# Five seven-product units in seven of ten gate and up half-pairs, their loop written out, and first loads in another order

## The chip, the cores and the metric

The kernel runs on one core of one Trainium2 chip. The metric is the device time of one launch in microseconds (us). The engines are named as in the profile: PE is TensorE, DVE is VectorE, ACT is ScalarE, POOL is GpSimd, and SP is SyncE, which here only issues DMAs.

## What is computed

One residual block on x of 256 tokens by 2048 features, all in float32:

```python
f = swiglu(rmsnorm(h, ffn1_pre_g), ffn1_w_gate, ffn1_w_up, ffn1_w_down)   # 2048 -> 5632 -> 2048
h = h + 0.5 * rmsnorm(f, ffn1_post_g)
u = rmsnorm(h, mix_pre_g)
z = u @ w_in                                  # 2048 -> 5120: lru_x, lru_gate, sc_b, sc_c, sc_x
xc = causal_dwconv(lru_x, conv_w, conv_b)
y_lru = rg_lru(xc, w_r, b_r, w_i, b_i, lam) * gelu(lru_gate)   # 8 heads: w_r, w_i are 128x128 each
y_sc = sc_b * causal_dwconv(sc_c * sc_x, sc_conv_w)
h = h + rmsnorm(concat(y_lru, y_sc) @ w_out, mix_post_g)
h = h + 0.5 * rmsnorm(swiglu(rmsnorm(h, ffn2_pre_g), ...), ffn2_post_g)
```

where `swiglu(x) = (silu(x @ w_gate) * (x @ w_up)) @ w_down`. All matrices are read from the chip's memory once.

## The kernel before

**Precision.** A float32 product is made of three matmuls: each operand is split into a rounded part (hi, made by ACT as a cast) and the rest (lo, made by DVE as raw minus hi), and `three` (L1735, L1736, L1737) adds hi·hi, hi·lo and lo·hi in one bank. So each weight that reaches PE has had one ACT pass and one DVE pass.

**Gate and up.** Of the 11 column chunks of 512, chunk 0 is done plainly (`first_chunk`, `group`). The other 10 chunks are five pairs. A pair of 1024 columns is done for w_gate (a "half", c even) and then for w_up (c odd): HALVES = 10 halves, c = 0 to 9. A half has GP = 8 units, p = 0 to 7; a unit is 2 row blocks (of 128) by 2 column blocks (of 512) of weights, times 2 token blocks. This 2x2x2 block product is done either plainly, with 8 products, so 24 matmuls, or by the Winograd form of Strassen's scheme with 7 products, so 21 matmuls ("seven-product unit"). `SEVEN[c]` lists the units of half c that are done with seven.

A seven-product unit needs three more weight blocks, U2, V4 and V3, which are sums of the raw ones. They cost two DVE instructions (`half_sums`, L1220 and L1222), an ACT cast (`sums_hi`, L824) and a DVE subtraction (`sums_lo`, L1228). One of the raw blocks is a sum of two, which POOL makes by an accumulating DMA (`pair_sums`, L675).

**Order on DVE** in a half (`half_steps`): the seven bank sums that empty the last half's PSUM banks (`bank_sums`), `half_lo` of unit 1; then for each unit in turn `half_sums` if it is a seven, `half_lo` (L1207), `sums_lo` if it is a seven. In an even half (c = 2, 4, ...) `pair_hidden` of the previous pair lies between `half_sums` and `half_lo` of units 2 and 4 (L1172, two instructions). At the end it does unit 0 of the next half. Three waits tie DVE to PE: `half_sums` waits until PE is through with the seven-product unit two before it (`two_back`, since the sums have two buffers), `bank_sums` waits for the last matmuls of the half, and in even halves ACT's cast `sums_hi` of unit 6 lies behind two PSUM copies (`pair_copy`) of transposes that PE does after units 3 to 6 (`pair_transpose`, 4 transposes each).

**Buffers.** The raw, hi and lo weights have four places; unit p uses place p % 4. Places 0 and 1 (`u_raw0`) lie where the ring of the plain chunks lay, places 2 and 3 (`u_raw1`) where `resid` lay. So in half 0 the loads of units 0 and 1 wait for `lo_ready` of the plain chunk's late groups, and those of units 2 and 3 for the squares of all blocks of `resid` (`blk_sq`) and, in the second FFN, for its copy to memory (`resid_kept`).

**Loops.** Half 0 and half 9 are written out. Halves 1 to 8 are a hardware loop on each of SP, ACT, DVE and PE: `Fori` with two turns, TURN = 4 halves in each turn. Waits in it are on register values.

**Mixer.** The columns of w_in are 10 chunks of 8 groups (`load_chunk`), each group one 512 KB load in a ring of four slots. SP issues loads in the order of its program; before the second chunk (q == 1) it waits for `fg_done` (the gains of the first FFN's last bank), then loads the gain row of the mixer's norm, broadcast to 1 MB (`gpost`), and the heads w_r and w_i (512 KB each). The heads are first used on PE at chunk 3, group 6; the gain in the output projection.

Of the kernel before, what the change touches and what calls it, by code (L numbers as in the profile page):

```python
# [22 lines left out]
def hybrid_block_kernel(nc, x, f1_pre, f1_wg, f1_wu, f1_wd, f1_post, mix_pre, w_in, conv_w, conv_b,  # L23
# [67 lines left out]

# [3 lines left out]
    TURN = 4  # L95
    SEVEN = [(2, 4, 6)] + [(0, 2, 3, 4, 6) if c % 2 else (0, 2, 4, 6) for c in range(1, HALVES)]
# [3 lines left out]
    turn_sevens = first_seven[1 + TURN] - first_seven[1]  # L100
# [20 lines left out]
    assert FC == 2 * PAIRS + 1 and HALVES == 2 + 2 * TURN and NS % 2 == turn_sevens % 2 == 0  # L121
# [16 lines left out]
    def lin(q, a, b):  # L138

        it, c = q  # L140
        return a * c + b if isinstance(it, int) else it * (TURN * a) + (a * c + b)
# [10 lines left out]
    with ctx:  # L152
# [241 lines left out]
        def turns(q, a, b):  # L394

            it, c = q
            return b if isinstance(it, int) else it * a + b

# [3 lines left out]
        def seven_count(f, q, p):  # L402
            return turns(q, turn_sevens, NS * f + seven_place(q, p) + 1)

        def sums_count(f, q, p, back=0):
            return turns(q, 2 * turn_sevens, 2 * (NS * f + seven_place(q, p) + 1) - back)
# [4 lines left out]
        def pair_count(f, q, p):  # L411
            units = [p in SEVEN[c] for c in range(HALVES)]
            return turns(q, 16 * sum(units[1:1 + TURN]), 16 * (sum(units) * f + sum(units[:q[1] + 1])))
# [4 lines left out]
        def raw_count(f, q, p):  # L418
            halves = [sum(raw_loads(c, p % 4 + 4)) for c in range(HALVES)]
            return turns(q, sum(halves[1:1 + TURN]),  # L420
                         sum(halves) * f + sum(halves[:q[1]]) + sum(raw_loads(q[1], p)))
# [48 lines left out]
        def _(sync):  # L470
# [25 lines left out]
            def ffn(f):  # L496
# [15 lines left out]
                with sync.Fori(0, (HALVES - 2) // TURN) as it:  # L512
                    for c in range(1, 1 + TURN):
                        load_half(f, (w_gate, w_up)[c % 2], (it, c))
# [34 lines left out]
            def load_half(f, w, q):  # L549
                it, c = q  # L550
                for p in range(GP):
                    if q[1] == 0 and p < 4:
# [9 lines left out]
                    def cols(b, n):  # L562
                        return (slice(first + b * W, first + b * W + n * W) if isinstance(it, int)
                                else ds(it * (TURN * W) + (first + b * W), n * W))
# [18 lines left out]

            X_LOADS = ((0, 1), (2,), (3,), (4, 5, 6, 7), (), (), (), ())
            ffn(0)
            for q, (kind, jc) in enumerate(Z):
                if q == 1:
                    sync.wait_ge(fg_done, TOK * NC)
                    load_gain(mix_post)
                    sync.wait_ge(w_used, starts["in"])  # L590
# [1430 lines left out]
```

## Time and profile before

| | us |
|---|---|
| runs of the kernel | 1741.73, 1742.92, 1745.69; median 1742.92 |
| the profiled execution's own time | 1742.19 |
| its span, first to last instruction | 1740.2 |
| PE busy | 1716.8 |
| DVE busy | 1460.6 |
| ACT busy | 993.1 |
| granted PE clock | 0.999 |

Busy times are unions of the instructions' spans. A matmul's end is modelled: one of 128x512 stands as 0.39 us long, while the next one starts 0.23 us after it, so "busy" includes overlap, and the distance between starts is the time that a matmul takes of PE.

### The profile page before, as it was taken

Reading aid. Unit: us, or ns where it says so; the run is one execution under the profiler, and the core shown is the slowest. Engines: PE = TensorE matmul, PEld = TensorE weight load, DVE = VectorE, ACT = ScalarE, POOL = GpSimd, SP = SyncE. Lnnn points to the kernel's source line nnn. Section 1 sums busy time; section 2 is a strip of 40 time slices with the busy share of each in tenths; the row PEclk is TensorE's granted clock in tenths of the full one; section 3 lists DMA queues with packets and bytes.
Section 4 is the critical chain, followed back from the end, with each engine's and each line's share of the span. In section 5 each row is a group of like instructions: output and inputs, shape, how many; then the busy total and the mean of one; then the engine's idle time right before and its main releaser. Section 6 shows DMA issues by size and latency. Waiting matters only on the chain.

```text
span 1740.2 us, 21509 instructions
## 1 busy us (share of the span) xinstructions
PE 1716.8 (99%) x7712; PEld 1417.0 (81%) x7712; DVE 1460.6 (84%) x1286; ACT 993.1 (57%) x951; POOL 183.5 (11%) x175
## 2 busy tenths in 40 slices
PE   8999999999999999999999999999999999999998
PEld 6788888888888888788888878788888888888886
DVE  6899999999989877755685558999989999989787
ACT  6665656555656454656654447565656565755453
POOL 5210000000000000100000018011010111000010
PEclk9999999999999999999999999999999999999999
DMA  7788878787767688665565656887877787677775
GB/s 233 229 230 234 227 227 242 221 241 219 227 198 235 221 231 265 197 205 175 163 194 180 194 181 226 231 241 227 237 224 228 232 233 233 194 227 229 227 226 206
DMA packets 150825, 382.38 MB, mean 220 GB/s; under 512 B 12620, under 2 KB 14804, under 8 KB 149972
## 3 DMA queue, kind: packets, MB, share of 16 engines
q1 hardware_dynamic: 133716, 350.33, 61.9%
q0 software_dynamic: 16992, 30.94, 11.3%
q8 instruction: 49, 0.80, 0.2%
q14 instruction: 36, 0.29, 0.1%
q10 hardware_dynamic: 32, 0.01, 0.0%
HBM read 377.03 MB, written 4.19 MB: 219 GB/s over the span
## 4 chain that ended last, share of the span: by engine, by line
PE 90%; DVE 3%; POOL 2%; DMA 2%; issue 1%; ACT 1%; DVEq 0%; SPq 0%; ACTq 0%
PE ps L1735 22%; PE ps L1737 22%; PE ps L1736 22%; PE ps L1633 7%; PE ps L1635 7%; PE ps L1634 7%; PE ps L1730 1%; POOL x L638 1%; DVE u_lo L1207 1%; DMA u_raw<-in_ffn_w_gate 1%; DVE w_lo L1090 1%; DMA raw<-in_w_in 1%; DMA u_raw<-in_ffn_w_up 1%; PE ps L1944 1%; DVE tsum L1222 0%
## 5 line engine op out<-in xcount | busy, mean ns | idle before, releaser
L817 ACT CAST u_hi<-u_raw 128x2048 fp32r<-128x2048 f32 x160 | 305.9, 1912 | 167.2 <-DMA u_raw<-in_ffn_w_gate 87.8
L1207 DVE TENSOR_TENSOR u_lo<-u_raw,u_hi 128x2048 fp32r<-128x2048 f32 x160 | 366.4, 2290 | 9.2 <-ACT u_hi L817 5.3
L1090 DVE TENSOR_TENSOR w_lo<-raw,w_hi 128x1024 fp32r<-128x1024 f32 x156 | 199.8, 1288 | 135.1 <-ACT w_hi L718 132.9
L718 ACT CAST w_hi<-raw 128x1024 fp32r<-128x1024 f32 x160 | 166.6, 1051 | 139.5 <-PE ps L1635 112.3
L1735 PE MATMUL ps<-u_hi,xT_hi 128*128 128x512 f32 x608 | 236.8, 390 | 0.0
L1737 PE MATMUL ps<-u_hi,xT_lo 128*128 128x512 f32 x608 | 236.8, 389 | 0.0
L1736 PE MATMUL ps<-u_lo,xT_hi 128*128 128x512 f32 x608 | 236.6, 389 | 0.0
L979 ACT CAST d_hi<-d_raw 128x2048 fp32r<-128x2048 f32 x80 | 153.0, 1912 | 117.9 <-DMA d_raw<-in_ffn_w_down 117.9
L1420 DVE TENSOR_TENSOR d_lo<-d_raw,d_hi 128x2048 fp32r<-128x2048 f32 x80 | 183.0, 2289 | 18.4 <-ACT d_hi L979 15.1
L824 ACT CAST t_hi<-tsum 128x1536 fp32r<-128x1536 f32 x88 | 130.6, 1484 | 102.4 <-DVE tsum L1222 101.5
L1633 PE MATMUL ps<-w_hi,xT_hi 128*128 128x512 f32 x448 | 179.1, 400 | 4.2 <-DVE xT_lo L1128 3.2
L1735 PE MATMUL ps<-d_hi,hT_all 128*128 128x512 f32 x460 | 179.1, 389 | 0.0
L1737 PE MATMUL ps<-d_hi,hT_all 128*128 128x512 f32 x460 | 179.0, 389 | 0.0
L1736 PE MATMUL ps<-d_lo,hT_all 128*128 128x512 f32 x460 | 178.9, 389 | 0.0
L1635 PE MATMUL ps<-w_hi,xT_lo 128*128 128x512 f32 x448 | 175.3, 391 | 0.0
L1634 PE MATMUL ps<-w_lo,xT_hi 128*128 128x512 f32 x448 | 175.1, 391 | 0.0
L1228 DVE TENSOR_TENSOR t_lo<-tsum,t_hi 128x1536 fp32r<-128x1536 f32 x88 | 154.2, 1752 | 20.7 <-ACT t_hi L824 20.7
L1736 PEld LDWEIGHTS ps<-u_lo,xT_hi 128*128 128x128 f32 x608 | 114.1, 188 | 24.1
L1737 PEld LDWEIGHTS ps<-u_hi,xT_lo 128*128 128x128 f32 x608 | 114.1, 188 | 24.1
L1735 PEld LDWEIGHTS ps<-u_hi,xT_hi 128*128 128x128 f32 x608 | 114.1, 188 | 24.0
L1735 PE MATMUL ps<-u_hi,xf 128*128 128x512 f32 x320 | 128.7, 402 | 3.9 <-DVE u_lo L1207 3.6
L1737 PE MATMUL ps<-u_hi,xf 128*128 128x512 f32 x320 | 124.9, 390 | 0.0
(203 smaller groups left out, 3039.9 us busy)
## 6 DMA issues: line engine op xcount, KB each, us to landing
d_raw<-in_ffn_w_down SPq DMA_DIRECT2D x50, 1024.0 KB, 6.8
u_raw<-in_ffn_w_gate SPq DMA_DIRECT2D x42, 1024.0 KB, 5.2
raw<-in_w_in SPq DMA_DIRECT2D x80, 512.0 KB, 3.7
u_raw<-in_ffn_w_up SPq DMA_DIRECT2D x30, 1024.0 KB, 5.1
u_raw<-in_ffn_w_up SPq DMA_DIRECT2D x100, 256.0 KB, 4.1
u_raw<-in_ffn_w_up SPq DMA_DIRECT2D x50, 512.0 KB, 3.7
u_raw<-in_ffn_w_gate SPq DMA_DIRECT2D x76, 256.0 KB, 4.3
u_raw<-in_ffn_w_gate SPq DMA_DIRECT2D x38, 512.0 KB, 3.7
```

The lines of the kernel that those rows point to most:

```text
L718: sc.copy(w_hi[:, s], raw[:, s]).then_inc(hi_ready, 1)
L817: sc.copy(unit(u_hi, p), unit(u_raw, p)).then_inc(unit_hi, 1)
L1090: ve.tensor_tensor(w_lo[:, s], raw[:, s], w_hi[:, s].bitcast(f32), ALU.subtract).then_inc(lo_ready, 1)
L1207: ve.tensor_tensor(unit(u_lo, p), unit(u_raw, p), unit(u_hi, p).bitcast(f32), ALU.subtract).then_inc(unit_lo, 1)
L1228: ve.tensor_tensor(t_lo[:, u], tsum[:, u], t_hi[u][:].bitcast(f32), ALU.subtract).then_inc(t_lo_done, 1)
L1420: ve.tensor_tensor(d_lo[n][:], d_raw[n][:], d_hi[n][:].bitcast(f32), ALU.subtract).then_inc(d_lo_done, 1)
L1633: te.matmul(dst, xh, w_hi[:, s, k], start=start and k == 0, stop=False)
L1634: te.matmul(dst, xh, w_lo[:, s, k], start=False, stop=False)
L1635: last = te.matmul(dst, xl, w_hi[:, s, k], start=False, stop=stop and k == GK - 1)
L1735: te.matmul(dst, xs[0], hi, start=start, stop=False)
L1736: te.matmul(dst, xs[0], lo, start=False, stop=False)
L1737: return te.matmul(dst, xs[1], hi, start=False, stop=stop)
```

## The change

The list of seven-product units is another one: halves 2 and 6 keep four, half 0 keeps three, and the other seven have five (before, only odd halves had five). In each FFN two more units, unit 3 of halves 4 and 8, are done with seven products. With that, the four `Fori` loops over halves 1 to 8 are written out as Python loops, and the register arithmetic (`turns`, `lin`) falls away. In half 0 SP issues the loads of units 2 and 3 ahead of those of units 0 and 1. In the mixer the heads are loaded one at a time, at group 4 of chunk 1 and group 2 of chunk 2, and the gain row at the start of chunk 3.

```diff
     PAIRS = (FC - 1) // 2
     HALVES = 2 * PAIRS
     UNITS = HALVES * GP
-    TURN = 4
-    SEVEN = [(2, 4, 6)] + [(0, 2, 3, 4, 6) if c % 2 else (0, 2, 4, 6) for c in range(1, HALVES)]
+    SEVEN = [(2, 4, 6)] + [(0, 2, 4, 6) if c in (2, 6) else (0, 2, 3, 4, 6) for c in range(1, HALVES)]
...
     def lin(q, a, b):
-        it, c = q
-        return a * c + b if isinstance(it, int) else it * (TURN * a) + (a * c + b)
+        return a * q[1] + b
...
         def seven_count(f, q, p):
-            return turns(q, turn_sevens, NS * f + seven_place(q, p) + 1)
+            return NS * f + seven_place(q, p) + 1
...
                 load_half(f, w_gate, (0, 0))
-                with sync.Fori(0, (HALVES - 2) // TURN) as it:
-                    for c in range(1, 1 + TURN):
-                        load_half(f, (w_gate, w_up)[c % 2], (it, c))
+                for c in range(1, HALVES - 1):
+                    load_half(f, (w_gate, w_up)[c % 2], (0, c))
                 load_half(f, w_up, (0, HALVES - 1))
...
             def load_half(f, w, q):
                 it, c = q
-                for p in range(GP):
-                    if q[1] == 0 and p < 4:
+                for p in ((2, 3, 0, 1, 4, 5, 6, 7) if c == 0 else range(GP)):
+                    if c == 0 and p < 4:
                         old = Place(starts[f"up{f + 1}"])
                         if p < 2:
                             sync.wait_ge(lo_ready, old.count(2 * GP - 3 + 2 * p))
...
+            HEADS_LOAD = {(1, 4): (0, w_r), (2, 2): (1, w_i)}
             X_LOADS = ((0, 1), (2,), (3,), (4, 5, 6, 7), (), (), (), ())
             ffn(0)
             for q, (kind, jc) in enumerate(Z):
-                if q == 1:
-                    sync.wait_ge(fg_done, TOK * NC)
-                    load_gain(mix_post)
-                    sync.wait_ge(w_used, starts["in"])
-                    for m, w in enumerate((w_r, w_i)):
+                for j in range(GP):
+                    if (q, j) in HEADS_LOAD:
+                        m, w = HEADS_LOAD[q, j]
+                        sync.wait_ge(w_used, starts["in"])
                         sync.dma_start(w_ri[:, m], w[0].rearrange("h d e -> d h e")).then_inc(heads_in, 16)
-                load_chunk(Place(starts["in"] + GP * q), w_in_v, Z_COL[kind] // W + jc, range(GP))
+                    elif (q, j) == (3, 0):
+                        sync.wait_ge(fg_done, TOK * NC)
+                        load_gain(mix_post)
+                    load_chunk(Place(starts["in"] + GP * q), w_in_v, Z_COL[kind] // W + jc, [j])
...
-                with dve.Fori(0, (HALVES - 2) // TURN) as it:
-                    for c in range(1, 1 + TURN):
-                        half_steps(f, (it, c))
+                for c in range(1, HALVES - 1):
+                    half_steps(f, (0, c))
```

ACT's and PE's loops are written out in the same way as DVE's, and the other counters lose their `turns` as `seven_count` does.

## Rows read from the trace of the kernel before

**Rows 1.** Page, part 1: busy us (share of the span), instructions.

```profile
PE 1716.8 (99%) x7712; PEld 1417.0 (81%) x7712; DVE 1460.6 (84%) x1286; ACT 993.1 (57%) x951; POOL 183.5 (11%) x175
```

**Rows 2.** Timeline, TensorE (start us, us): first matmuls of two units, transposes between.

```profile
205.70 0.39 PE L1735 MATMUL ps<-u_hi,xf 128*128 128x512 f32 x1
...
246.50 0.60 PE L1730 MATMUL ps<-ident,hid 128*128 128x128 f32 x4
246.86 0.48 PE L1735 MATMUL ps<-u_hi,xf 128*128 128x512 f32 x1
```

**Rows 3.** Timeline, VectorE, from one even unit 4 to the next half's.

```profile
203.23 2.29 DVE L1207 TENSOR_TENSOR u_lo<-u_raw,u_hi 128x2048 fp32r<-128x2048 f32 x1
205.44 1.75 DVE L1228 TENSOR_TENSOR t_lo<-tsum,t_hi 128x1536 fp32r<-128x1536 f32 x1
207.10 2.28 DVE L1207 TENSOR_TENSOR u_lo<-u_raw,u_hi 128x2048 fp32r<-128x2048 f32 x1
209.31 0.69 DVE L1220 TENSOR_TENSOR tsum<-u_raw 128x512 f32<-128x512 f32 x1
...
211.29 2.29 DVE L1207 TENSOR_TENSOR u_lo<-u_raw,u_hi 128x2048 fp32r<-128x2048 f32 x1
...
241.93 2.29 DVE L1207 TENSOR_TENSOR u_lo<-u_raw,u_hi 128x2048 fp32r<-128x2048 f32 x1
```

**Rows 4.** Timeline, VectorE: its longest idle time; a unit behind the loop.

```profile
254.47 1.76 DVE L1228 TENSOR_TENSOR t_lo<-tsum,t_hi 128x1536 fp32r<-128x1536 f32 x1 [2.20 <-ACT t_hi L824]
...
449.82 0.69 DVE L1220 TENSOR_TENSOR tsum<-u_raw 128x512 f32<-128x512 f32 x1 [0.24 <-PE ps L1737]
...
451.88 2.29 DVE L1207 TENSOR_TENSOR u_lo<-u_raw,u_hi 128x2048 fp32r<-128x2048 f32 x1
```

**Rows 5.** Timeline, TensorE, unit 4 of half 1, first FFN.

```profile
122.67 0.50 PE L1735 MATMUL ps<-u_hi,xf 128*128 128x512 f32 x1 [0.56 <-DVE u_lo L1207]
```

**Rows 6.** Timeline at the loop's turn: TensorE at both ends of half 5 in either FFN; ScalarE; VectorE.

```profile
268.83 0.39 PE L1735 MATMUL ps<-u_hi,xT_hi 128*128 128x512 f32 x1
...
308.98 0.39 PE L1735 MATMUL ps<-u_hi,xT_hi 128*128 128x512 f32 x1
...
1293.31 0.39 PE L1735 MATMUL ps<-u_hi,xT_hi 128*128 128x512 f32 x1
...
1335.09 0.39 PE L1735 MATMUL ps<-u_hi,xT_hi 128*128 128x512 f32 x1
...
1294.34 1.91 ACT L817 CAST u_hi<-u_raw 128x2048 fp32r<-128x2048 f32 x1 [4.29 <-DMA u_raw<-in_ffn_w_up]
...
1294.52 0.69 DVE L1251 TENSOR_TENSOR act_x<-ps,act_x 128x512 f32<-128x512 f32 x1 [1.44 <-issue]
```

**Rows 7.** First loads of half 0: SP, ScalarE, VectorE, TensorE; DMA's GB/s in slices of 0.275 us.

```profile
41.48 0.37 SPq L475 DMA_DIRECT2D raw<-in_ffn_w_up  x1
47.41 0.37 SPq L581 DMA_DIRECT2D u_raw<-in_ffn_w_gate  x1
...
39.06 0.18 ACT L754 ACTIVATION_READ_ACCUMULATOR act_g<-resid 128x1 f32 x1
...
52.74 1.92 ACT L817 CAST u_hi<-u_raw 128x2048 fp32r<-128x2048 f32 x1 [3.87 <-PE ps L1635]
...
66.10 0.69 DVE L1220 TENSOR_TENSOR tsum<-u_raw 128x512 f32<-128x512 f32 x1 [2.38 <-DMA u_raw<-in_ffn_w_gate]
...
70.50 0.50 PE L1735 MATMUL ps<-u_hi,xf 128*128 128x512 f32 x1 [0.95 <-DVE u_lo L1207]
...
GB/s 0 0 0 0 0 179 45 149 268 283 328 417 432 402 417 402 402 387 380 462 454 402 402 410 380 402 447 462 402 402 417 447 417 387 402 283 179 171 216 179
```

**Rows 8.** Timeline at the second input chunk: SP, ScalarE, TensorE.

```profile
722.08 0.34 SPq L478 DMA_DIRECT2D gpost<-in_mix_post_g  x1
...
732.93 1.05 ACT L718 CAST w_hi<-raw 128x1024 fp32r<-128x1024 f32 x1 [2.68 <-DMA raw<-in_w_in]
...
735.29 0.50 PE L1633 MATMUL ps<-w_hi,xT_hi 128*128 128x512 f32 x1 [0.82 <-DVE w_lo L1090]
```

More of the change, by code:

```diff
@@ L120, in hybrid_block_kernel @@
     EVAC = 7
-    assert FC == 2 * PAIRS + 1 and HALVES == 2 + 2 * TURN and NS % 2 == turn_sevens % 2 == 0
+    assert FC == 2 * PAIRS + 1 and HALVES == 10 and NS % 2 == 0
     DU = GF - SLOTS
@@ L392, in unit_count @@
             return lin(q, GP, UNITS * f + p + 1)
-        def turns(q, a, b):
-            it, c = q
-            return b if isinstance(it, int) else it * a + b
         def seven_place(q, p):
@@ L402, in seven_count @@
         def seven_count(f, q, p):
-            return turns(q, turn_sevens, NS * f + seven_place(q, p) + 1)
+            return NS * f + seven_place(q, p) + 1
         def sums_count(f, q, p, back=0):
-            return turns(q, 2 * turn_sevens, 2 * (NS * f + seven_place(q, p) + 1) - back)
+            return 2 * (NS * f + seven_place(q, p) + 1) - back
         def seven_sem(q, p):
@@ L412, in pair_count @@
             units = [p in SEVEN[c] for c in range(HALVES)]
-            return turns(q, 16 * sum(units[1:1 + TURN]), 16 * (sum(units) * f + sum(units[:q[1] + 1])))
+            return 16 * (sum(units) * f + sum(units[:q[1] + 1]))
         def raw_loads(c, p):
@@ L419, in raw_count @@
             halves = [sum(raw_loads(c, p % 4 + 4)) for c in range(HALVES)]
-            return turns(q, sum(halves[1:1 + TURN]),
-                         sum(halves) * f + sum(halves[:q[1]]) + sum(raw_loads(q[1], p)))
+            return sum(halves) * f + sum(halves[:q[1]]) + sum(raw_loads(q[1], p))
         def two_back(f, q, p):
@@ L562, in cols @@
                     def cols(b, n):
-                        return (slice(first + b * W, first + b * W + n * W) if isinstance(it, int)
-                                else ds(it * (TURN * W) + (first + b * W), n * W))
+                        return slice(first + b * W, first + b * W + n * W)
                     raw_u = unit(u_raw, p)
@@ L780, in pair_copy @@
                 first = MC * (1 + 2 * i + k)
-                if not isinstance(it, int):
-                    r, first = it * (TURN * TOK) + r, it * (TURN * MC) + first
                 hidden_copy(f, r, src, first, t)
@@ L903, in ffn @@
                 half_steps(f, (0, 0))
-                with act.Fori(0, (HALVES - 2) // TURN) as it:
-                    for c in range(1, 1 + TURN):
-                        half_steps(f, (it, c))
+                for c in range(1, HALVES - 1):
+                    half_steps(f, (0, c))
                 half_steps(f, (0, HALVES - 1), True)
@@ L1315, in ffn @@
                     softplus("end")
-                with dve.Fori(0, (HALVES - 2) // TURN) as it:
-                    for c in range(1, 1 + TURN):
-                        half_steps(f, (it, c))
+                for c in range(1, HALVES - 1):
+                    half_steps(f, (0, c))
                 last = (0, HALVES - 1)
@@ L1841, in ffn @@
                 half_steps(f, (0, 0))
-                with pe.Fori(0, (HALVES - 2) // TURN) as it:
-                    for c in range(1, 1 + TURN):
-                        half_steps(f, (it, c))
+                for c in range(1, HALVES - 1):
+                    half_steps(f, (0, c))
                 last = (0, HALVES - 1)
```

1 line of the change is left out of this document (removed).

## The prediction, made before the changed kernel ran

> **What bounds the kernel now.** The page first: PE is busy 99% of the span and DVE 84% [rows 1]. That share of DVE is a mean over unlike stages, so the stages that the change touches are read in the timeline, for both engines. On PE one looks for starts: unit 4 of half 3 starts at 205.70 and unit 4 of half 4 at 246.86 [rows 2]. Between them lie 41.16 us, in which PE does 180 matmuls (the rest of half 3, 21+24+21+24, and units 0 to 3 of half 4, 21+24+21+24) and four transposes, which take 0.36 us (246.50 to 246.86). So a matmul costs 0.2267 us, and there is no gap: in this stage PE sets the pace, at the full clock of 2.4 GHz (the granted share is 0.999).
>
> Then DVE in the same stretch: `half_lo` of unit 4 starts at 203.23 in half 3 and at 241.93 in half 4 [rows 3], 38.70 us apart, and the timeline shows no idle time of DVE between. So DVE has full work there, and it is the faster engine by only 41.16 - 38.70 = 2.46 us. How far it is ahead: `u_lo` of unit 4 ends at 205.52 in half 3, 0.18 us ahead of PE's need, and at 244.22 in half 4, 2.64 us ahead. DVE's longest idle time of the pair, 2.20 us, comes only after that, ahead of unit 6's `t_lo` [rows 4]. DVE can't carry its slack over: in an odd half `half_sums` of unit 4 has to wait for PE's end of unit 2 (a wait of 0.24 us in half 9) [rows 4], so every odd half puts the lead back to 0.1 to 0.2 us at unit 4.
>
> **The change, part by part.**
>
> Fewer matmuls: unit 3 of halves 4 and 8 in two FFNs, four units, 3 matmuls each: 12 x 0.2267 = 2.7 us less on PE.
>
> More work on DVE in the same four places. A seven-product unit adds `t_lo` (205.44 to the next start at 207.10, 1.66 us) and the pair of `tsum` (209.31 to 211.29, 1.98 us) [rows 3], so 3.64 us, all of it between `half_lo` of units 2 and 4, where DVE has no idle time. The lead at unit 4 of half 4 becomes 2.64 - 0.68 (PE comes sooner) - 3.64 = -1.68 us: PE waits. Written out, the code is a bit slower: behind the loop `tsum` to `u_lo` takes 451.88 - 449.82 = 2.06 us [rows 4], not 1.98. Three or four such pairs in the stretch, and a start from 0.12 instead of 0.18, make it -2.0. Bounds of the stall: 1.7 us (in-loop durations) and 2.1 (all with the longer one and 0.05 us from DVE's end to PE's start). I take 2.0, because half 9 shows what written-out code takes: 4 x 2.0 = +8.0 us (bounds 6.8 and 8.4). The same arithmetic fits a stall that is in the trace: in half 1 of the first FFN, where DVE starts late behind small work for the softplus, PE waits at unit 4 for `u_lo`, 0.56 us [rows 5].
>
> Where this stall goes: PE is late by 2.0 us, and so is all that waits for PE. DVE then stands at a lead of 0.05 instead of 2.64, but has its idle 2.20 us ahead of it in this half [rows 4] and some 0.25 us at unit 0, so it enters half 5 about where it does now (5.6 us ahead at unit 0). POOL's additional accumulating DMA is issued when PE leaves half 3, and in even halves DVE comes to unit 3 later than in odd ones, by the 1.2 us of `pair_hidden`; ACT is busy 57% [rows 1]. Both are in time where odd halves are.
>
> The other odd halves, now written out: the lead at unit 4 falls from 0.18 to 0.12, and a matmul that is fed in the last moment takes up to 0.1 us more (0.50 against 0.39 as it stands in [rows 2, 5]). Seven halves more at 0.07: +0.5 us (bounds 0 and 0.7).
>
> The loops' turn, between halves 4 and 5. In the second FFN ACT's cast stands 4.29 us idle and DVE stands 1.44 us in the midst of its bank sums, waiting for nothing that the profile shows [rows 6]. The first lies at the branch, so I read both as code that had to be fetched. Half 5 then takes PE 1335.09 - 1293.31 = 41.78 us against 308.98 - 268.83 = 40.15 us in the first FFN [rows 6], where its 177 matmuls alone are 40.13. Without the loop: -1.6 us in the second FFN, nothing in the first (bounds 0, if written-out code waits as much elsewhere, and 1.6). The Trainium skill (Runtime: NRT & Kernel Launch, "Instruction fetch mechanics") says that instructions stream in sequence and that a taken branch out of the window that is held forces a fetch before work goes on. The trace agrees in the second FFN and not in the first, whose turn costs nothing; by the rule alone both turns would cost, and the saving would be twice 1.6.
>
> First loads. In half 0 PE stands 0.95 us idle ahead of unit 2, because `half_sums` of unit 2 waited 2.38 us for its load [rows 7]. A matmul's span is 0.16 longer than its pitch and the first after a wait 0.1 slower, so this costs 1.2 us. SP has issued the last plain load at 41.48 and then waits until 47.41 for unit 0's buffer, while the squares that unit 2's buffer waits for end at about 39.2 [rows 7]. So units 2 and 3 (2 MB) are issued at about 42, POOL can add its part when its forms are done, at 51.3, and unit 2 is there by 57: its stall goes. Against it, unit 0's 1 MB now stands behind 2 MB. DMA moves about 400 GB/s when it is full [rows 7], 2.6 us for 1 MB: the last plain load lands near 46, then units 2, 3 and 0 at 48.5, 51 and 53.7. ACT casts unit 0 at 52.74 [rows 7], so it is 0.9 late, with 0.8 us of lead to cover it and a stall of 0.4 at unit 1 behind it that takes in the rest; 0.2 comes through. Net -1.0 us (bounds -1.4 and +1). In the second FFN unit 2 has no stall and unit 1's (1.4 us) comes from a late norm on POOL, which stays and covers a late unit 0: 0 (bounds 0 and +1).
>
> Mixer. SP's gain and heads are issued at 722.08, 2 MB ahead of chunk 1's first group, whose cast then waits 2.68 us for its load, and PE stands 0.82 idle [rows 8], with 0.16 and 0.1 as above 1.1 us. Afterwards they come one by one, each ahead of a load that is issued four slots (10.9 us) early: `w_ri` takes about 2.8 us of DMA, the gain row 2.6 to 4.8, and a load lands some 4 us before its cast there. -1.1 us (bounds -1.1 and 0, if the gain uncovers a wait as long).
>
> Sum: -2.7 + 8.0 + 0.5 - 1.6 - 1.0 + 0 - 1.1 = +2.1 us on the profiled execution's own 1742.19, so 1744.3. That execution (span 1740.2, with 2.0 us around it) stands 0.7 below the median of the runs, 1742.92; on the median the forecast is 1745.0. A measurement of this kernel can tell 0.2%, 3.5 us, so "same" is 1739.4 to 1746.4.
>
> **Rivals.**
> A: the additional work on DVE is hidden, and halves 4 and 8 run at PE's pace. For it: DVE has 4 us idle in each pair of halves, more than 3.64. Against it: that idle lies behind unit 4. Time: 1742.9 - 2.7 + 0.5 - 1.6 - 1.0 - 1.1 = 1737.0, faster. Chance 0.16.
> B, slower: the lag isn't made up in the even half, and odd halves 5 and 9 start unit 0 with a lead of 4.4 us, as half 4 does, not 5.6. From there on DVE has no slack up to unit 4, which comes 0.3 to 0.4 us late. It decides once the lead at unit 0 is below 5.0. Four places at 0.4: 1746.6. Against it: the 2.20 us of idle. Chance 0.14.
> C: the new order of loads doesn't do what it says: unit 0 comes late by more than its cover, and the mixer's wait only moves to chunk 3. Sum without -1.0 and -1.1, and +1: 1748.1. Chance 0.10.
> D: the turn's cost comes back as fetches in the written-out code. 1746.6. Chance 0.05.
> E: the first FFN's turn costs as much as the second's, so that twice 1.6 go. 1743.4. Against it: the 40.15 us of its half 5 hold no wait [rows 6]. Chance 0.01. It is what the page of the Trainium skill named above would have.
>
> **How the numbers follow.** The forecast, 1745.0, has 0.54; its own range is 1743 to 1746.5. With A below, and C above, 8 in 10 lie between 1739.0 and 1748.5. Faster: A and a small tail, 0.18. Slower: C, half of B and D, and the upper tail of the forecast, 0.24. Same: 0.58.
>
> **What would show it.** PE's wait for `u_lo` at unit 4 of halves 4 and 8 in both FFNs, 1.7 to 2.1 us each, four long waits where there were none. The wait at unit 2 of half 0 in the first FFN gone. No wait at chunk 1 of the mixer, half 5 of the second FFN some 40.2 us long, 12 matmuls fewer. DVE's idle 2.20 at unit 6 of halves 4 and 8 gone. Wrong would be: no wait at those units (A), or waits at unit 4 of halves 5 and 9 as well (B).

## The result, and the profile after

The changed kernel took 1751.33 us (median of 12 runs, 1748.19 to 1755.81) against 1744.18 for the kernel before in the same comparison: ratio 1.0045, 95% interval 1.0037 to 1.0053. It is slower by 7.2 us where 2.1 were forecast, and lies outside the range that was given. The profiled execution took 1751.38, with a span of 1749.4.

From the page of the kernel after, parts 1 and 3 (queue: packets, MB, share of 16 engines):

```profile
PE 1716.6 (98%) x7700; PEld 1414.7 (81%) x7700; DVE 1472.8 (84%) x1298; ACT 998.6 (57%) x955; POOL 185.9 (11%) x179
...
q0 software_dynamic: 17568, 31.99, 11.9%
q8 instruction: 60, 0.98, 0.2%
```

TensorE does 12 matmuls fewer than in [rows 1] and is busy for as long; the 9 us that its span grew by are idle time. Its waits after, by the line that waited and what released it (us in total, times, longest):

```profile
PE ps L1722 <- DVE u_lo L1195: 9.8, 10, 1.4
...
PE ps L1722 <- issue: 2.0, 2, 1.2
...
PE ps L1722 <- DVE d_lo L1407: 1.1, 1, 1.1
PE ps L1620 <- DVE w_lo L1078: 0.2, 1, 0.2
```

Line numbers are smaller by 9 to 14 than before: `three` is L1722 to L1724, `half_lo` L1195, `down_lo` L1407, `w_lo` L1078. Where the waits lie, in the timeline of TensorE after:

```profile
59.87 0.47 PE L1722 MATMUL ps<-u_hi,xf 128*128 128x512 f32 x1 [1.23 <-issue]
...
66.75 0.50 PE L1722 MATMUL ps<-u_hi,xf 128*128 128x512 f32 x1 [1.15 <-DVE u_lo L1195]
...
249.39 0.50 PE L1722 MATMUL ps<-u_hi,xf 128*128 128x512 f32 x1 [1.44 <-DVE u_lo L1195]
...
555.84 0.47 PE L1722 MATMUL ps<-d_hi,hT_all 128*128 128x512 f32 x1 [1.14 <-DVE d_lo L1407]
...
1089.79 0.50 PE L1722 MATMUL ps<-u_hi,xf 128*128 128x512 f32 x1 [1.16 <-DVE u_lo L1195]
...
1272.23 0.50 PE L1722 MATMUL ps<-u_hi,xf 128*128 128x512 f32 x1 [1.17 <-DVE u_lo L1195]
...
1301.15 0.39 PE L1722 MATMUL ps<-u_hi,xT_hi 128*128 128x512 f32 x1
...
1341.33 0.39 PE L1722 MATMUL ps<-u_hi,xT_hi 128*128 128x512 f32 x1
...
1605.28 0.47 PE L1722 MATMUL ps<-d_hi,hT_all 128*128 128x512 f32 x1 [0.78 <-issue]
```

Four kinds of place are to be seen here.

- 249.39 is unit 4 of half 4: the forecast stall. It stands at all four places (starts 249.39, 417.13, 1279.16, 1446.53), each about 1.7 us by the starts of the matmuls around it, with 0.1 to 0.4 more at unit 3. From half 4 or 8 to the next half's start TensorE takes 1.27, 1.51, 2.48 and 1.55 us more than before, although it has three matmuls (0.68 us) less to do.
- 59.87, 66.75 and 1089.79 are units 0 and 1 of half 0. The wait at unit 2 in [rows 7] is gone; two in the first FFN and one in the second stand where none was looked for. The one at 1089.79, unit 0 of the second FFN, takes the place of a wait at unit 1 that the kernel before has there (1.19 us idle at its 1090.47).
- 1301.15 and 1341.33 are both ends of half 5 in the second FFN: 40.18 us, against 41.78 in [rows 6]. In the first FFN half 5 takes 40.59 us (271.38 to 311.97), 0.4 more than in the kernels that have all loops written out and the old list of units (40.18 to 40.19).
- 555.84 lies in the down projection of the first FFN, 1272.23 at unit 3 of half 4 in the second. Neither stage showed such a wait before, and nobody had touched the down projection. A second one in the down projections is at 1605.28.

What ends these last waits shows on the other engines, after (SP, POOL, ScalarE, in order of time within each stretch):

```profile
43.91 11.37 SPq L569 DMA_DIRECT2D u_raw<-in_ffn_w_gate  x3
55.53 1.91 ACT L806 CAST u_hi<-u_raw 128x2048 fp32r<-128x2048 f32 x1 [6.10 <-DMA u_raw<-in_ffn_w_gate]
...
544.25 0.86 POOL L674 DMA_DIRECT2D d_raw<-in_ffn_w_down  x1 [10.62 <-DMA d_raw<-in_ffn_w_down]
544.52 0.38 SPq L521 DMA_DIRECT2D d_raw<-in_ffn_w_down  x1
551.34 1.91 ACT L967 CAST d_hi<-d_raw 128x2048 fp32r<-128x2048 f32 x1 [5.92 <-DMA d_raw<-in_ffn_w_down]
...
1260.32 0.87 POOL L666 DMA_DIRECT2D u_raw<-in_ffn_w_gate  x1 [5.70 <-DMA u_raw<-in_ffn_w_gate]
1260.90 0.33 SPq L565 DMA_DIRECT2D u_raw<-in_ffn_w_gate  x1
1267.83 1.91 ACT L806 CAST u_hi<-u_raw 128x2048 fp32r<-128x2048 f32 x1 [4.16 <-DMA u_raw<-in_ffn_w_gate]
```

The first pair: SP's three issues between 43.91 and 55.3 are the loads of 1 MB of unit 3, unit 0 and unit 1 (at 43.91, 47.98 and 54.92). Unit 0's cast starts at 55.53; before it started at 52.74 [rows 7]. The second and third: POOL's accumulating transfer of 256 KB is issued 0.27 us ahead of SP's load of 1 MB (544.25 and 544.52), or 0.58 us ahead of SP's next loads (1260.32 and 1260.90), and the cast that needs it starts 7.1 and 7.5 us after it was issued. The median of such a transfer in the down projections is 4.2 us before and 4.6 after, from issue to landing.

### The profile page after: what moved, and what is told of

It is laid out like the page before. It is cut to its first block, busy times and chain, and to the rows that moved or that the text cites. A ratio compares the mean times of both kernels' runs of the same rounds, so it can differ in the third digit from the quotient of the medians.

```text
span 1749.4 us, 19821 instructions
## 1 busy us (share of the span) xinstructions
PE 1716.6 (98%) x7700; PEld 1414.7 (81%) x7700; DVE 1472.8 (84%) x1298; ACT 998.6 (57%) x955; POOL 185.9 (11%) x179
## 4 chain that ended last, share of the span: by engine, by line
PE 84%; DVE 8%; DMA 5%; issue 2%; ACT 1%; POOL 0%; DVEq 0%; SPq 0%; ACTq 0%
PE ps L1722 20%; PE ps L1724 20%; PE ps L1723 20%; PE ps L1620 7%; PE ps L1622 7%; PE ps L1621 7%; DMA u_raw<-in_ffn_w_gate 3%; DVE u_lo L1195 3%; DVE t_lo L1216 1%; PE ps L1717 1%; DVE w_lo L1078 1%; DVE tsum L1210 1%; DMA d_raw<-in_ffn_w_down 1%; DVE tsum L1208 1%; PE ps L1930 0%
## 5 line engine op out<-in xcount | busy, mean ns | idle before, releaser
L1195 DVE TENSOR_TENSOR u_lo<-u_raw,u_hi 128x2048 fp32r<-128x2048 f32 x160 | 366.1, 2288 | 14.9 <-ACT u_hi L806 7.2
L1078 DVE TENSOR_TENSOR w_lo<-raw,w_hi 128x1024 fp32r<-128x1024 f32 x156 | 198.0, 1275 | 134.7 <-ACT w_hi L709 132.8
L1722 PE MATMUL ps<-u_hi,xT_hi 128*128 128x512 f32 x592 | 230.6, 390 | 0.0
L1724 PE MATMUL ps<-u_hi,xT_lo 128*128 128x512 f32 x592 | 230.5, 389 | 0.0
L1723 PE MATMUL ps<-u_lo,xT_hi 128*128 128x512 f32 x592 | 230.4, 389 | 0.0
L813 ACT CAST t_hi<-tsum 128x1536 fp32r<-128x1536 f32 x92 | 136.7, 1486 | 120.8 <-DVE tsum L1210 120.5
L1407 DVE TENSOR_TENSOR d_lo<-d_raw,d_hi 128x2048 fp32r<-128x2048 f32 x80 | 182.9, 2288 | 14.6 <-ACT d_hi L967 11.4
L1722 PE MATMUL ps<-d_hi,hT_all 128*128 128x512 f32 x460 | 179.3, 390 | 1.9 <-DVE d_lo L1407 1.1
L1724 PE MATMUL ps<-d_hi,hT_all 128*128 128x512 f32 x460 | 179.0, 389 | 0.0
L1216 DVE TENSOR_TENSOR t_lo<-tsum,t_hi 128x1536 fp32r<-128x1536 f32 x92 | 161.1, 1751 | 12.8 <-ACT t_hi L813 12.8
L1722 PE MATMUL ps<-u_hi,xf 128*128 128x512 f32 x320 | 129.4, 404 | 11.3 <-DVE u_lo L1195 9.8
L1722 PEld LDWEIGHTS ps<-u_hi,xT_hi 128*128 128x128 f32 x592 | 111.2, 188 | 23.4
L1724 PEld LDWEIGHTS ps<-u_hi,xT_lo 128*128 128x128 f32 x592 | 111.1, 188 | 23.4
L1724 PE MATMUL ps<-u_hi,xf 128*128 128x512 f32 x320 | 124.9, 390 | 0.0
```

The lines of the kernel that those rows point to most:

```text
L1078: ve.tensor_tensor(w_lo[:, s], raw[:, s], w_hi[:, s].bitcast(f32), ALU.subtract).then_inc(lo_ready, 1)
L1195: ve.tensor_tensor(unit(u_lo, p), unit(u_raw, p), unit(u_hi, p).bitcast(f32), ALU.subtract).then_inc(unit_lo, 1)
L1216: ve.tensor_tensor(t_lo[:, u], tsum[:, u], t_hi[u][:].bitcast(f32), ALU.subtract).then_inc(t_lo_done, 1)
L1407: ve.tensor_tensor(d_lo[n][:], d_raw[n][:], d_hi[n][:].bitcast(f32), ALU.subtract).then_inc(d_lo_done, 1)
L1722: te.matmul(dst, xs[0], hi, start=start, stop=False)
L1723: te.matmul(dst, xs[0], lo, start=False, stop=False)
```

## The experiments

All times are medians of 11 or 12 runs, but for `loads_back` (9), `heads_back` (5) and `adds_with_loads` (4). The kernel before took 1744.01 us in the first group of experiments (those with one part undone and `only_written_out`), 1743.94 in the second (`before_loads`, `before_heads`, `hidden_later`, `adds_with_loads`), 1743.66 in the third (`sp_written_out`, `act_dve_written_out`, `heads_act_dve`, `heads_act_dve_unit2_early`) and 1743.90 in the fourth (`pe_written_out`, `all_but_pe_written_out`, `heads_all_written_out`). An interval reaches about 0.09% to either side, 1.6 us (0.13% with 5 runs, 0.15% with 4); a difference between two experiments is less certain than either.

### The changed kernel with one part undone

`sevens_back`, the old list of seven-product units:

```diff
-    SEVEN = [(2, 4, 6)] + [(0, 2, 4, 6) if c in (2, 6) else (0, 2, 3, 4, 6) for c in range(1, HALVES)]
+    SEVEN = [(2, 4, 6)] + [(0, 2, 3, 4, 6) if c % 2 else (0, 2, 4, 6) for c in range(1, HALVES)]
```

> The changed kernel with the list of seven-product units as it was before (four in every even half); everything else as changed. Theory S (the two new units in halves 4 and 8 are the greater part of the loss, because DVE comes too late at unit 4): the profile of the changed kernel lost 1.3, 1.5, 2.5 and 1.6 us in these four halves, so this one is 6 to 7 us faster than the changed kernel, about 1744 to 1745, and no wait of PE at units 3 and 4 of halves 4 and 8 is left. Rival U (the written-out code itself is slower, through fetches or slower waits on all engines): within 2 us of the changed kernel, 1749 to 1751.

Measured: 1746.25 us, ratio 1.0013 [1.0003, 1.0022]. The two more units per FFN cost 1751.33 - 1746.25 = 5.1 us; the forecast had 8.0 - 2.7 = 5.3, and the expectation above 6 to 7. The stall and its size were right, and so Rival A is out. The profile of the changed kernel has two waits in the down projections, of 1.3 and 0.9 us by the starts, that need not be the two units' doing: this kernel's own profile has one there too, with POOL's and SP's issues 0.23 us apart.

```profile
1664.98 0.50 PE L1722 MATMUL ps<-d_hi,hT_all 128*128 128x512 f32 x1 [1.83 <-DVE d_lo L1407]
...
1666.96 0.63 PE L1722 MATMUL ps<-d_hi,xg 128*128 128x512 f32 x1
1667.39 0.63 PE L1723 MATMUL ps<-d_lo,xg 128*128 128x512 f32 x1
...
1666.00:1669.00 3.00, 3.00 (x8) 2.32 (x8) 2.80 (x2) 1.90 (x1) 0.00 (x0) 0.50 0.84 323
```

This wait costs 2.0 us by the starts, and then something that the forecast doesn't have: behind it the granted clock of TensorE falls to 0.50, that is from 2.4 to 1.2 GHz (the last row is a stretch with its length, the busy times of TensorE, its weight loads, VectorE, ScalarE and GpSimd, then the granted clock, DMA's share and GB/s). Eight matmuls start 0.43 us apart instead of 0.23, another 1.6 us. So one meeting of POOL's transfer with a large load can cost 3.7 us.

`loads_back`, half 0 loads units 0 to 7 in order again:

```diff
-                for p in ((2, 3, 0, 1, 4, 5, 6, 7) if c == 0 else range(GP)):
+                for p in range(GP):
```

> The changed kernel with the loads of half 0 in the order 0 to 7 again. Theory L (unit 0's load now stands behind 2 MB, and PE waits at units 0 and 1 in both FFNs): from the two profiles, 1.1 us in the first FFN and 0.5 in the second come back, so 1.5 us faster than the changed kernel, about 1749.8; PE's waits at units 0 (1.3 us each) are gone, and the one at unit 2 of the first FFN (0.95) is back. Rival (the late unit 0 only takes in waits that come anyway, from a late start or a late norm): no difference, under 0.5 us.

Measured: 1748.85, ratio 1.0030 [1.0021, 1.0040]. So the new order costs 2.5 us where 1.0 of gain was forecast. In the two profiled executions it costs 1.4 us in half 0 of the first FFN and nothing in that of the second, by the starts of the same matmuls; where the rest of the 2.5 lies is not shown.

`heads_back`, gain row and heads loaded ahead of chunk 1 again (the diff of the mixer shown above, reversed).

> The changed kernel with gain row and heads loaded ahead of the mixer's second chunk again. Theory M (the move takes away the wait of PE at that chunk and nothing else): 1.1 us slower than the changed kernel, 1752.4, with 0.8 us idle ahead of the chunk's first matmul. Rival (the gain row at chunk 3 costs as much): no difference.

Measured, with 5 runs: 1750.94, ratio 1.0038 [1.0025, 1.0051]: 0.4 us below the changed kernel where 1.1 above it was expected, and less than the comparison can tell. Its profile has no wait at chunk 1.

### The kernel before with one part of the change

`only_written_out`: all four loops written out, nothing else.

> The kernel before with only its loops over halves 1 to 8 written out: old list of units, old order of loads, gain and heads at their old place. By the row of the loop's turn in the second FFN: 1.6 us faster than before less 0.5 for unit 4 of the odd halves, so 1743.0 against 1744.2. Rival U (written-out code costs): slower than before, by up to 5 us, with longer or more waits of PE for d_raw and u_raw in the down projections and halves than the kernel before has.

Measured: 1744.57, ratio 1.0006 [0.9997, 1.0015], where -1.1 us had been forecast. The single runs spread from 1741.57 to 1749.61; the kernel before's go from 1741.78 to 1746.52. The turn's 1.6 us are gone in its trace as they should be, and yet the median is not below before's. (The profiled execution, 1741.57, is the shortest of the eleven, so its trace doesn't show what the others lose.) This is the first thing that the forecast's steps can't explain; it is taken up under "Which loop costs".

`before_loads`, the new order of loads alone:

```diff
-                for p in range(GP):
+                for p in ((2, 3, 0, 1, 4, 5, 6, 7) if q[1] == 0 else range(GP)):
```

> The kernel before, with only the loads of half 0 in the new order (2, 3, 0, 1, 4 to 7). Theory L (unit 0 is 1.3 us late in both FFNs, and the wait at unit 2 of the first FFN goes): 0.5 to 2.5 us slower than before, 1744.5 to 1746.5, with waits of PE at unit 0 of 1 us and more in both FFNs. My prediction had 1 us faster, 1743.0.

Measured: 1745.26, ratio 1.0008 [0.9999, 1.0017], 1.3 us above before, not clear of noise by itself. In its timeline SP issues the first load for unit 2 at 42.21 and TensorE waits at unit 1:

```profile
43.67 11.37 SPq L581 DMA_DIRECT2D u_raw<-in_ffn_w_gate  x3
...
65.38 0.50 PE L1735 MATMUL ps<-u_hi,xf 128*128 128x512 f32 x1 [1.30 <-DVE u_lo L1207]
...
1087.33 0.50 PE L1735 MATMUL ps<-u_hi,xf 128*128 128x512 f32 x1 [2.16 <-DVE u_lo L1207]
```

In the second FFN the wait is at unit 0 (1087.33): in both FFNs a wait was replaced by one at the unit ahead of it (before, they were at unit 2 and at unit 1). In half 0 of the first FFN the two are worth the same; in that of the second this execution loses 1.5 us.

`before_heads`, the later heads and gain alone.

> The kernel before, with only the gain row and the heads loaded later. As predicted: 1.1 us faster, 1742.9. Rival (the wait at chunk 1 is there in some runs only, since it hangs on 0.8 us of SP's wait for `fg_done`): 0 to 0.5 us faster, and no new wait.

Measured: 1742.66, ratio 0.9992 [0.9983, 1.0001]: 1.3 us less than before, as forecast (1.1). TensorE's wait for `w_lo` falls from 0.8 us to this:

```profile
PE ps L1635 <- DVE w_lo L1092: 0.2, 1, 0.2
```

`hidden_later`: the changed kernel with the old order of loads, and `pair_hidden` moved behind `half_lo` of units 4 and 5, so that VectorE reaches unit 4 of halves 4 and 8 earlier; the PSUM copies and transposes of the pair follow one unit later.

```diff
-                    if c and c % 2 == 0 and 3 <= p < 3 + 2 * TOK:
-                        pair_transpose(f, q, p - 3, XB)
+                    if c and c % 2 == 0 and 4 <= p < 4 + 2 * TOK:
+                        pair_transpose(f, q, p - 4, XB)
```

> The changed kernel with the loads of half 0 in the old order, and in even halves DVE's two instructions of `pair_hidden` one after `half_lo` of unit 4 and one after that of unit 5; PE's transposes come one unit later and ACT's copies of them later too. Same work. Theory S (PE waits at unit 4 of halves 4 and 8 because DVE has 18.3 us of work in a row that all lies ahead of that unit): the 2.2 us that `pair_hidden` takes leave that stretch, the waits of 1.65 us fall under 0.5, and the time falls by 4 to 6 us against the changed kernel with the old order of loads (1748.9), so 1743 to 1745. Rival (DVE is simply full over the whole pair of halves, and the wait only moves to units 5 to 7): 1748 to 1749, with waits of the same sum at other units.

Measured: 1746.75, ratio 1.0017 [1.0008, 1.0026], 2.1 us below the changed kernel with the old loads (1748.85), where 4 to 6 were expected. The waits at unit 4 of halves 4 and 8 fall from 1.7 to about 0.3 us in three of the four places (in half 4 of the second FFN 0.87 is left), but TensorE now waits at unit 4 of halves 5 and 9:

```profile
289.03 0.50 PE L1726 MATMUL ps<-u_hi,xf 128*128 128x512 f32 x1 [0.45 <-DVE u_lo L1199]
...
455.47 0.50 PE L1726 MATMUL ps<-u_hi,xf 128*128 128x512 f32 x1 [0.46 <-DVE u_lo L1199]
```

At unit 0 of half 5 VectorE is only 3.9 us ahead instead of 5.8. The work was put off, not hidden: with five seven-product units in both halves of a pair VectorE has hardly any idle time left (1.5 us from unit 4 of half 3 to unit 4 of half 5 in the first FFN, against 3.9 in the kernel before).

### The accumulating transfer beside a large load

`adds_with_loads`: the kernel before, with POOL's transfer in the down projection held back to the moment at which SP issues its 1 MB.

```diff
                     pool.wait_ge(d_b12[n], d_pairs(f, g))
+                    if g < DS[-1]:
+                        pool.wait_ge(d_used, d_count(f, g - 3))
```

> The kernel before, with one more wait on POOL in the down projections: its accumulating DMA of a seven-product unit is issued only when PE has left the unit that SP waits for as well, so that it falls together with SP's 1 MB load of the next unit. 26 of 30 of them. Theory C (an accumulating DMA that is issued within 0.5 us of a 1 MB load takes 6 to 8 us to land, not 4.3, because its packets come behind that load's): median of its landing times over 6 us in both down projections, and PE waits 1 to 3 us at each such unit: 20 to 60 us slower. Rival (only its own delay of about 1 us counts): landing times stay at 4 to 5 us, and the kernel is under 5 us slower, as DVE is 2 us ahead there.

Measured: 1772.99, ratio 1.0158 [1.0143, 1.0174]. POOL issues at 555.52, 0.51 us behind SP's load; the third row is the median of all 30 from issue to landing, the last TensorE's waits:

```profile
555.01 0.38 SPq L532 DMA_DIRECT2D d_raw<-in_ffn_w_down  x1
555.52 0.86 POOL L685 DMA_DIRECT2D d_raw<-in_ffn_w_down  x1 [10.21 <-PE ps L1739]
...
d_raw<-in_ffn_w_down POOLq DMA_DIRECT2D x30, 256.0 KB, 6.5
...
PE ps L1737 <- DVE d_lo L1422: 18.6, 20, 2.1
```

This is as expected. So the two together take the transfer from 4.2 to 6.5 us, 20 waits of about 1 us follow, and the two down projections take 28.5 us more together. The waits at 555.84 and 1272.23 of the changed kernel are single cases of the same: in the down projections of the kernel before, POOL's issue is 0.8 us or more ahead of SP's 1 MB, 1.9 in the median; after, the median is 1.6, and two of 30 are under 0.5.

### Which loop costs

`sp_written_out` and `act_dve_written_out`: SyncE's loop alone, or ScalarE's and VectorE's.

```diff
-                with sync.Fori(0, (HALVES - 2) // TURN) as it:
-                    for c in range(1, 1 + TURN):
-                        load_half(f, (w_gate, w_up)[c % 2], (it, c))
+                for c in range(1, HALVES - 1):
+                    load_half(f, (w_gate, w_up)[c % 2], (0, c))
```

> The kernel before with only SyncE's pair loop written out; VectorE, ScalarE and TensorE keep their loops. It asks where the cost of writing out sits. Theory 1, the cost is SyncE's: with its code written out, its loads of 1 MB in the down projections follow GpSimd's accumulating transfer more closely and the 256 KB loads ahead of them take 3.5 to 3.6 us instead of 3.2 to 3.3; the median gap between GpSimd's issue and the load falls from 1.86-1.93 us to about 1.6, and the time is 1743.5 to 1745.5 with the loop's turn of the second FFN (1.6 us) still paid. Theory 2, the cost isn't SyncE's but that of the engines that compute: gap and load times stay as before, and the time is within 0.7 us of before's.

> The kernel before with the pair loops of ScalarE and VectorE alone written out; SyncE and TensorE keep theirs. Theory 1 (the turn is ScalarE's and VectorE's, the cost is SyncE's): the half after the turn in the second FFN takes 40.2 us instead of 41.8, the down projections' gaps between GpSimd's issue and the load of 1 MB stay at 1.9 us in the median, and the time is 1.6 us below before, 1742.4. Theory 2 (the turn's 1.6 us is given back at the next wait for a load, whoever is written out): the half shortens and the time stays, 1743.6 to 1744.4. Theory 3: writing TensorE out was what took the turn away; the half stays at 41.8 us, and the time at before's.

Measured: 1742.48, ratio 0.9995 [0.9986, 1.0004], and 1742.39, ratio 0.9992 [0.9983, 1.0001]. SyncE's code is not what costs: with it written out the gap between POOL's issue and SP's load keeps its median of 1.9 us, though in this one execution a pair of them met (0.24 us apart) and made a wait of 1.7 us. Neither time can be told from before's by itself. But the turn belongs to ScalarE and VectorE: with their loops written out, half 5 of the second FFN takes 1334.59 - 1294.40 = 40.19 us, and with SyncE's alone it still took 41.35.

```profile
1294.40 0.39 PE L1733 MATMUL ps<-u_hi,xT_hi 128*128 128x512 f32 x1
...
1334.59 0.39 PE L1733 MATMUL ps<-u_hi,xT_hi 128*128 128x512 f32 x1
```

`pe_written_out` and `all_but_pe_written_out`, the same edit on TensorE's loop alone, and on the other three engines' alone:

> The kernel before with TensorE's pair loop alone written out. Theory 1, TensorE's code is the cost: the page shows 60 transfers of instructions in queue q8, as in the kernels with all loops written out, against 49 of before and of the kernels where TensorE keeps its loop; the 256 KB loads ahead of GpSimd's transfers in the down projections take 3.5 to 3.6 us (3.2 to 3.3 before), the gap to the load of 1 MB falls to about 1.6 us, and the time is 1 to 2 us above before's. Theory 2, the cost is of all loops together (less wait at the turn lets every transfer draw nearer to the next): load times and gaps as before, and the time within 0.7 us of before's.

> The kernel before with the loops of SyncE, ScalarE and VectorE written out, TensorE's kept. Theory 1: load times and gaps of before, 49 transfers of instructions, and 1.3 to 1.6 us below before. Theory 2: as with all four written out, 0 to 1 us above before, with 256 KB loads of 3.5 to 3.6 us.

Measured: 1745.71, ratio 1.0012 [1.0003, 1.0021], and 1742.20, ratio 0.9989 [0.9980, 0.9998]. TensorE's code written out costs 1.8 us, the other three's gains 1.7; both are just clear of noise. From the page and the list of DMAs, first with TensorE's loop written out:

```profile
q8 instruction: 60, 0.98, 0.2%
...
d_raw<-in_ffn_w_down SPq DMA_DIRECT2D x60, 256.0 KB, 4.3
...
d_raw<-in_ffn_w_down POOLq DMA_DIRECT2D x30, 256.0 KB, 4.4
```

and with the other three written out:

```profile
q8 instruction: 49, 0.80, 0.2%
...
d_raw<-in_ffn_w_down SPq DMA_DIRECT2D x60, 256.0 KB, 4.2
...
d_raw<-in_ffn_w_down POOLq DMA_DIRECT2D x30, 256.0 KB, 4.2
```

All eight kernels with TensorE's loop written out show 60 transfers of instructions, the nine in which it is kept 49. For the same 30.94 MB the share of queue q0, POOL's, is 11.5 to 11.6% in the former and at most 11.4% in the latter. In the down projections, the 256 KB load that POOL's transfer waits for takes 3.5 to 3.6 us in the median in all eight and 3.2 to 3.3 in the others (`adds_with_loads` aside), so POOL issues later and nearer to SP's 1 MB: 1.5 to 1.7 us ahead of it, not 1.9. The median over all 60 of the 256 KB loads tells less: it is 4.3 us in `sp_written_out` too.

In the profiled execution of `pe_written_out` no such pair met in the down projections. What it loses to a load lies between halves 3 and 4 of the first FFN. First the kernel before, then `pe_written_out`:

```profile
202.34 0.86 POOL L675 DMA_DIRECT2D u_raw<-in_ffn_w_up  x1 [9.10 <-DMA u_raw<-in_ffn_w_up]
207.21 1.91 ACT L817 CAST u_hi<-u_raw 128x2048 fp32r<-128x2048 f32 x1 [0.68 <-DMA u_raw<-in_ffn_w_up]
...
205.79 0.86 POOL L675 DMA_DIRECT2D u_raw<-in_ffn_w_up  x1 [11.90 <-DMA u_raw<-in_ffn_w_up]
210.79 1.91 ACT L817 CAST u_hi<-u_raw 128x2048 fp32r<-128x2048 f32 x1 [3.66 <-DMA u_raw<-in_ffn_w_up]
...
228.12 0.50 PE L1735 MATMUL ps<-u_hi,xT_hi 128*128 128x512 f32 x1 [0.57 <-DVE hid L1245]
```

The 256 KB load that POOL waits for took 7.9 us here and 5.0 before, the cast comes 3.6 us later (0.6 of it from this execution's later start), and TensorE loses 1.4 us by the starts. The runs also spread more: 1744.21 to 1749.41, against 1740.96 to 1743.20 with the other three written out.

How 11 more transfers of instructions, 0.18 MB in 382, go with slower loads isn't shown. They don't lie beside the loads of the down projections: between 435 and 690 us both `before` and `pe_written_out` have 9. The additional ones lie in the loop's second turn, halves 5 to 8, where the kernel before has none at all (none from 250 to 435 us, against 7).

The clock may have a part in it. The mean granted clock of each execution is on record, and one fall as in `sevens_back` takes 0.001 from it. It is 0.997 or less in 1 of the 114 executions of the kernel before and in none of the 55 of the five kernels that keep both TensorE's loop and the order of loads, but in 15 of the 104 of the ten kernels in which one of these two was changed. No trace of those executions was kept except `heads_act_dve_unit2_early`'s, so this is a hint and not shown.

### Better versions

`heads_act_dve`: the kernel before with heads and gain later, and ScalarE's and VectorE's loops written out.

> The kernel before with the norm weight and the heads' weights loaded later and the loops of ScalarE and VectorE written out; every half keeps its six-product units as before, and the first loads their order. If the two gains add: 1.3 us (heads later on the kernel before) and 1.6 us (the turn), so 1741.1, ratio 0.9983. If the turn is given back as it was with all loops written out: 1742.7, ratio 0.9993.

Measured: 1741.25, ratio 0.9988 [0.9979, 0.9997], the lowest of all, 2.4 us below before and 10 below the changed kernel. Each gain by itself had been 1.3. (The expectation says "six-product units"; the units are the seven-product ones of the kernel before.)

`heads_all_written_out`, the same with all four loops written out:

> The kernel before with the norm weight and the heads' weights loaded later and all four loops written out. Theory 1 (TensorE's code costs about 2 us): 1.0 to 2.5 us above the 1741.25 us that the same kernel took with only ScalarE's and VectorE's loops written out, so about before's time, with 256 KB loads of 3.5 to 3.6 us. Theory 2 (what was seen with all loops written out was the spread between builds): within 0.8 us of 1741.25.

Measured: 1743.25, ratio 0.9997 [0.9988, 1.0006]. TensorE's and SyncE's code add 2.0 us, as the price of TensorE's code has it. The kernel differs from `sevens_back` (1746.25) in the order of the first loads alone, so here that order costs 3.0 us.

`heads_act_dve_unit2_early`, half 0's loads in the order 0, 2, 3, 1:

```diff
-                for p in range(GP):
+                for p in ((0, 2, 3, 1, 4, 5, 6, 7) if q[1] == 0 else range(GP)):
```

> As heads_act_dve, with the first half's loads in the order unit 0, 2, 3, 1, then 4 to 7: unit 0 stays first, so that only units 2 and 3 move ahead of unit 1. In the kernel before, TensorE waits at unit 2 of the first FFN for a load; with unit 0 moved back (the change's order) it waited 1.3 to 1.4 us at unit 0 and as much at unit 1. Theory 1 (it was unit 0's place that cost): the wait at unit 0 stays away, that at unit 2 goes, unit 1's load lands about 2 us later and makes a wait of 0 to 1 us in its place: 0.5 us below heads_act_dve. Theory 2 (any unit moved behind the others is late by what its load takes, as unit 1's was): a wait of 1.3 us or more at unit 1, and a time 0.5 to 1.5 us above heads_act_dve.

Measured: 1744.63, ratio 1.0007 [0.9998, 1.0016], 3.4 us above the same kernel with the old order. ScalarE gets unit 0 in time (52.88) and unit 1 ten microseconds later; TensorE then waits 3.37 us at unit 1:

```profile
62.75 3.70 ACT L819 CAST u_hi<-u_raw 128x2048 fp32r<-128x2048 f32 x2 [3.81 <-DMA u_raw<-in_ffn_w_gate]
...
67.03 0.50 PE L1735 MATMUL ps<-u_hi,xf 128*128 128x512 f32 x1 [3.37 <-DVE u_lo L1208]
```

The wait at unit 1 is Theory 2's, but the price is above its 0.5 to 1.5 us. A half of it is the clock: behind the wait the granted clock is 0.50 and eight matmuls start 0.43 us apart, 1.6 us more.

```profile
68.00:71.30 3.30, 3.30 (x9) 2.54 (x9) 3.20 (x3) 2.43 (x2) 0.00 (x0) 0.50 0.58 86
```

## Why the prediction was wrong, step by step

Four kernels form a chain from before to after, so the terms can be set beside each other in us:

| step | forecast | measured |
|---|---|---|
| loops written out | +0.5 - 1.6 = -1.1 | +0.6 (only_written_out) |
| heads and gain | -1.1 | -1.3 (heads_all_written_out less only_written_out) |
| first loads | -1.0 | +3.0 (sevens_back less heads_all_written_out) |
| two more seven-product units | -2.7 + 8.0 = +5.3 | +5.1 (after less sevens_back) |
| sum | +2.1 | +7.3 (1751.33 less 1744.01) |

**The stalls at unit 4: right.** Lead and price came out as worked out from [rows 2, 3]: 1.7 us and a bit more at unit 3, against 2.0 with bounds of 1.7 and 2.1. What was not in the sum is that POOL's one more transfer per half met SP's loads once (1272.23, 1.3 us by the starts).

**Odd halves and Rival B: right that the lag is made up.** VectorE enters half 5 with 5.8 us of lead. One of the four odd halves behind, half 5 of the first FFN, still takes 0.4 us more (also in `loads_back` and `heads_back`, 40.55); why only that one is open. The written-out odd halves cost 0.07 us each in the one that was compared (40.19 against 40.12), as taken.

**The turn: right in place and size, wrong in the balance.** Half 5 of the second FFN is 1.6 us shorter. But "written out" stood in the sum for one thing, the turn, while it is an edit of four engines. On ScalarE, VectorE and SyncE it gains 1.7 us; on TensorE it costs 1.8, a term that the sum put at nothing but the 0.5. Rival D had this sign with a chance of 0.05, and named fetches in the written-out code. What the traces show is not TensorE waiting for code but loads that land later; that these make up the whole 1.8 is not shown. The Trainium skill (Runtime: NRT & Kernel Launch, "Instruction fetch mechanics") holds full unrolling to be preferable since a taken branch breaks the prefetch. For ScalarE and VectorE half 5 of the second FFN agrees (40.19 against 41.78 us); for TensorE the runs don't (1745.71 against 1743.90).

**The first loads: the step that failed most.** The sum had -1.0, and the new order cost +2.5 (changed kernel), +3.0 (`heads_all_written_out`) and +1.3 (kernel before). The wait that was to vanish did vanish, 1.2 us. What failed is the price of what came in its place, 0.2. The forecast put unit 0's landing at 53.7 and its cast 0.9 us late. In the changed kernel it landed at 55.5 (cast 55.53, 2.8 late, of which 0.6 is this execution's later start): the last plain load landed at 47.05, not 46, and units 2 and 3 were through at 53.0, not 51. Unit 3's load, issued at 43.91, took 9.1 us, and unit 0's, issued at 47.98, 7.5 instead of the 5.0 before. The 400 GB/s that I reckoned with came late: the core moved 274 GB/s from 42 to 46 us, 343 to 48, and 366 to 396 from then to 54. In `before_loads` unit 0 landed at 53.99, as forecast, and made no wait in the first FFN.

I also left out that unit 1's own load could be late. TensorE waited at unit 1 in both kernels (not in `sevens_back`, where unit 0 alone waits, 1.5 us). Its load took 7.5 us in the changed kernel and 6.4 in `before_loads`, against 5.1 before. Standing behind unit 0's load explains little of that: that one had landed 0.7 us ahead of unit 1's issue in `before_loads`, and 0.6 behind it in the changed kernel. What is new beside it is POOL's accumulating transfer for unit 2, issued at 51.83 and landed at 56.74 (before, it was issued at 60.45, behind unit 1's load). In the second FFN of the changed kernel, where this transfer is issued 1.8 us behind unit 1's load, that load took 5.1 and unit 1 waited 0.15. That the transfer is the cause was not tested. The second FFN came out as forecast there (a late unit 0, covered by a wait that comes anyway), but not in `before_loads`.

Rival C had "late by more than its cover" at +1: it had the mechanism for the loads, not the size, and its other half, a mixer's wait that only moves, did not come.

**Heads and gain: right on the kernel before** (1.3 us less, forecast 1.1), 1.3 less with all loops written out, and not to be told from nothing on the changed kernel (0.4 us the other way, with 5 runs). The wait at chunk 1 isn't in every execution: in the profiles of `only_written_out` and `heads_back`, which load them as before did, it isn't there either.

**The range.** Its bounds had +1 for the loads in each FFN and 0 for the turn's gain at worst. The loads came out above that on the changed kernel (+2.5), and the written-out code, at +0.6, at the upper end of its two terms together (0.7 and 0). All upper bounds together give +8.4, which would have held the measured +7.2; the range took the terms as independent and stopped at +5.6. Both parts that failed make loads land later, in a kernel where TensorE's waits are made by transfers, which is a reason to let them fail together; that they do was not measured apart.

## What to carry to other kernels

A load that is moved ahead is paid by the loads behind it, so follow the order down to the first unit that has cover, beyond the first one that is overtaken, with the durations that loads have beside others and not with the highest rate of the core, and see which other transfers the move brings forward. "Writing a loop out" is one edit per engine: try each engine by itself, since here two engines had all the gain and a third gave it back. A wait of TensorE can cost more than its length, since the clock may fall behind it: read the granted clock behind each long wait. And before filling an engine's idle time, look where in the stage it lies: VectorE's 4 us per pair lay behind the unit that was late.

## What the runs showed of the hardware that was not expected

- POOL's accumulating transfer of 256 KB takes 4.2 us by itself in the down projections, and 6.5 in the median (up to 7.8) if a load of 1 MB is issued within about 0.5 us of it.
- TensorE's program written out, and nothing else, changes 49 to 60 transfers of instructions, the median of the 256 KB load that POOL's transfer waits for in the down projections from 3.3 to 3.6 us, and the time by +1.8 us. With the loop kept, its second turn goes with no transfer of instructions at all (250 to 435 us and 1270 to 1460).
- Behind a single wait TensorE's granted clock can fall from 1.0 to 0.50, with 1.6 us lost over eight matmuls: after 1.83 us idle in `sevens_back` (1664.98), 2.26 in `heads_back` (1090.87) and 3.37 in `heads_act_dve_unit2_early` (67.03), but not after 2.16 in `before_loads` (1087.33). These rows alone give no rule for when it falls.
- The loop's turn costs half 5 of the second FFN 1.6 us in the kernel before (1.2 with SyncE's loop written out, 2.2 with TensorE's; but 1.4, 1.9 and 2.2 in `before_loads`, `before_heads` and `adds_with_loads`, which touch no loop, so the spread is no effect of the edit), and half 5 of the first FFN nothing in any of them (40.12 to 40.14 us).
